# A streaming encoder step on one core: the first MLP matrix as seven block products, rounded sums on GpSimd

## The chip, the cores and the metric

The kernel runs on one core of a Trainium2 chip. The metric is the time of one execution on the device in microseconds (us), median of several runs. In this kernel TensorE multiplies, VectorE and ScalarE do the elementwise work and read TensorE's results from PSUM, GpSimd does elementwise work in SBUF alone, SyncE (SP) issues most transfers; GpSimd issues some.

## The reference

One layer: input LayerNorm, one large projection, a pooling branch and a stick-breaking attention branch, gates, an output projection, a LayerNorm, a squared-ReLU MLP, a last LayerNorm. 512 new frames and 64 frames of a running stream, 576 rows that matter in the MLP. The part that the change touches:

```python
h = _layer_norm(ALPHA * h + (mix @ w_out + b_out), ln1_g, ln1_b)                        # 576 x 1024
f = jnp.square(jax.nn.relu(h @ w_mlp1 + b_mlp1)) @ w_mlp2 + b_mlp2                      # 1024 -> 4096 -> 1024
h = _layer_norm(ALPHA * h + f, ln2_g, ln2_b)
```

## The kernel before

Everything is kept transposed: channels on the 128 partitions, rows along the free axis, in two halves of 288 columns. A float32 operand x is split into a rounded part `hi` (type fp32r, written by ScalarE as a copy or a square) and a remainder `lo` = x - hi (written by VectorE); a product is three matmuls, hi*hi, hi*lo, lo*hi. A **unit** is a block of 128 output channels of a matrix with 1024 input channels: 8 steps x 2 halves x 3 = 48 matmuls. Weight units (512 KB) come by SP into a ring `raw` of four, ScalarE rounds one into `whi`, VectorE writes `wlo`, two units ahead of TensorE at most.

The MLP has 32 hidden units. Each gives a relu (ScalarE, from the PSUM banks `lin`), a square (VectorE), a rounded square (ScalarE) and its remainder (VectorE). The kernel goes through three passes of 12, 12 and 8 units (`PASS_UNITS`). After each of the first two passes, `winograd(s)` multiplies the 12 fresh hidden units with their part of the second matrix: hidden units are taken in six pairs and columns in two halves, so that the hidden activations are 2 x 2 blocks B11, B12 (even unit), B21, B22 (odd unit), and the pair of output blocks costs seven block products instead of eight. The moving operands are B11, B21, B22 and four sums: V5 = B11 - B12, T3 = B22 - B12, V6 = -V5 - B22, V4 = -V6 - B21. The weights' sums are made by VectorE (`weight_sum`). There are four groups (output blocks g and g + 4) of seven products (`OPS`), each of 6 pairs x 3 = 18 matmuls of 288 columns. Results are added by VectorE from PSUM into `r2`, the residual (`add_op`). The last 8 hidden units keep plain `f_hi`, `f_lo`, and the closing stage multiplies them plainly with the last part of the second matrix (`last_products`, weights split by `split_end`), output block by output block, with the last LayerNorm in between.

Order is written out by hand, engine by engine; each engine runs its queue in order, and semaphores hold it where a result is not there. Names in the change: `f_lo_done` counts remainders of hidden operands, `s_hi` and `s_lo` rounded weights and their remainders for the block products, `op_done` finished products, `lo_split` remainders of weight units. SP waits for `s_lo` before it loads over a place. GpSimd sums for the LayerNorms and is idle from 412 us, when it has written two constants, until 759 us. The residual's base (`residual2`, ScalarE) is made between hidden units 4 to 11.

## Time and profile before

| | us |
|---|---|
| median of 3 runs | 806.76 (806.7 to 807.0) |
| span of the profiled execution | 806.8 |
| TensorE (PE) busy | 792.7, 98% |
| VectorE (DVE) busy | 508.3, 63% |
| ScalarE (ACT) busy | 391.6, 49% |
| GpSimd (POOL) busy | 124.7, 15% |

The profiled execution's own time is its span, from the first to the last instruction. Busy time is summed over the whole span; what bounds a stage is read from that stage. Matmuls overlap in the pipeline (a record of 0.30 us, a new one every 0.13 us), so stages are measured from first start to first start. "idle before" is time in which an engine waited just before a group, with what ended it.

### The profile page before, as it was taken

The numbers are of one execution on the slowest core, as the hardware profiler recorded it, in microseconds if no ns is written. First come the engines' busy times: TensorE is split into PE (matmuls) and PEld (weight loads), VectorE is DVE, ScalarE is ACT, GpSimd is POOL, SyncE is SP. The second block draws the span as 40 slices with busy tenths as digits, with TensorE's granted clock in tenths as the row PEclk, the third lists the DMA queues.
The fourth block names the chain that finished last, engine by engine and source line by source line (L and its number), as shares of the span: only waits on it lengthen the run. The fifth ranks groups of instructions, "written<-read, shape, count | busy, mean of one in ns | idle before, by whom it ended". The sixth has DMA issues, their size and how long they took to land.

```text
span 806.8 us, 14570 instructions
## 1 busy us (share of the span) xinstructions
PE 792.7 (98%) x5863; PEld 766.1 (95%) x5864; DVE 508.3 (63%) x857; ACT 391.6 (49%) x652; POOL 124.7 (15%) x170
## 2 busy tenths in 40 slices
PE   8999999999999999999999999999999999999995
PEld 6999899999989999999999999999999999999994
DVE  5833344754547377876877779775667977445644
ACT  4633345655655475562556663334455433345324
POOL 2100000472220110016720000000000000000356
PEclk9999999999999999999999999999999999999998
DMA  7732231112111121243302214222221422222203
GB/s 275 291 116 85 73 113 53 54 56 80 53 54 53 53 70 62 79 131 106 95 11 79 66 39 157 80 105 79 87 75 49 157 79 105 80 78 79 79 2 117
DMA packets 23034, 71.62 MB, mean 89 GB/s; under 512 B 2416, under 2 KB 6656, under 8 KB 22592
## 3 DMA queue, kind: packets, MB, share of 16 engines
q1 hardware_dynamic: 22016, 67.97, 25.8%
q0 software_dynamic: 544, 2.52, 0.9%
q8 instruction: 40, 0.66, 0.3%
q10 hardware_dynamic: 416, 0.33, 0.1%
q14 instruction: 18, 0.15, 0.1%
HBM read 65.96 MB, written 4.85 MB: 88 GB/s over the span
## 4 chain that ended last, share of the span: by engine, by line
PE 93%; ACT 2%; DVE 2%; issue 1%; DMA 1%; SPq 0%; DVEq 0%; ACTq 0%
PE lin L652 15%; PE lin L653 14%; PE lin L654 14%; PE z L1143 6%; PE z L1146 6%; PE z L1145 6%; PE z L908 3%; PE lin L1046 3%; PE lin L1047 2%; PE lin L1048 2%; PE lin L1164 2%; PE lin L1162 2%; PE lin L1163 2%; PE z L973 1%; PE z L654 1%
## 5 line engine op out<-in xcount | busy, mean ns | idle before, releaser
L652 PE MATMUL lin<-h_hi,whi 128*128 128x288 f32 (+1 forms) x832 | 247.5, 297 | 0.0
L653 PE MATMUL lin<-h_lo,whi 128*128 128x288 f32 (+1 forms) x832 | 245.9, 296 | 0.0
L654 PE MATMUL lin<-h_hi,wlo 128*128 128x288 f32 (+1 forms) x832 | 245.0, 294 | 0.0
L652 PEld LDWEIGHTS lin<-h_hi,whi 128*128 128x128 f32 x832 | 156.4, 188 | 1.3 <-issue 1.1
L654 PEld LDWEIGHTS lin<-h_hi,wlo 128*128 128x128 f32 x832 | 156.6, 188 | 0.0
L653 PEld LDWEIGHTS lin<-h_lo,whi 128*128 128x128 f32 x832 | 156.4, 188 | 0.1
L1872 DVE TENSOR_TENSOR wlo<-raw,whi 128x1024 fp32r<-128x1024 f32 x65 | 80.2, 1234 | 33.9 <-ACT whi L1237 29.0
L1237 ACT ACTIVATE whi<-raw 128x1024 fp32r<-128x1024 f32 x58 | 61.0, 1051 | 50.6 <-PE lin L654 32.6
L1659 ACT ACTIVATE relu_t<-lin,vecs 128x288 f32<-128x288 f32 x60 | 30.0, 500 | 91.5 <-PE lin L654 88.1
L2328 DVE TENSOR_TENSOR relu_sq<-relu_t 128x288 f32<-128x288 f32 x60 | 27.4, 456 | 64.4 <-ACT relu_t L1659 64.4
L1143 PE MATMUL z<-f_ops,whi 128*128 128x288 f32 x216 | 64.1, 297 | 0.0
L1146 PE MATMUL z<-f_ops,wlo 128*128 128x288 f32 x216 | 63.5, 294 | 0.0
L1145 PE MATMUL z<-f_ops,whi 128*128 128x288 f32 x216 | 63.1, 292 | 0.0
L1706 ACT ACTIVATE whi<-w_set 128x768 fp32r<-128x768 f32 x36 | 30.5, 846 | 52.2 <-PE z L1146 41.9
L2867 POOL TENSOR_TENSOR sum<-r 128x576 f32<-128x576 f32 x1 | 1.4, 1432 | 347.0 <-DVE r L2568 347.0
L1143 PEld LDWEIGHTS z<-f_ops,whi 128*128 128x128 f32 x216 | 40.6, 188 | 0.4 <-issue 0.4
L2475 DVE TENSOR_TENSOR wlo<-w_set,whi 128x768 fp32r<-128x768 f32 x36 | 34.4, 956 | 10.0 <-ACT whi L1706 9.9
L1145 PEld LDWEIGHTS z<-f_ops,whi 128*128 128x128 f32 x216 | 40.6, 188 | 0.0
L1146 PEld LDWEIGHTS z<-f_ops,wlo 128*128 128x128 f32 x216 | 40.5, 187 | 0.0
L2093 DVE SCALAR_TENSOR_TENSOR sa<-z,sa 128x512 f32<-128x512 f32 (+4 forms) x25 | 19.8, 794 | 25.6 <-ACT sa L1415 25.4
L1145 PE MATMUL z<-f_ops,third_hi 128*128 128x288 f32 x120 | 35.6, 297 | 0.0
L1146 PE MATMUL z<-f_ops,third_lo 128*128 128x288 f32 x120 | 35.6, 297 | 0.0
(360 smaller groups left out, 1920.3 us busy)
## 6 DMA issues: line engine op xcount, KB each, us to landing
raw<-w_stream SPq DMA_DIRECT2D x88, 512.0 KB, 3.5
w_set<-w_sets SPq DMA_DIRECT2D x32, 384.0 KB, 3.7
r<-x_t SPq DMA_DIRECT2D x8, 296.0 KB, 6.2
kcache<-k_cache SPq DMA_DIRECT2D x1, 2048.0 KB, 10.0
vcache<-v_cache SPq DMA_DIRECT2D x1, 2048.0 KB, 8.1
y<-r SPq DMA_DIRECT2D x8, 160.0 KB, 1.8
k_new<-k_t POOLq DMA_DIRECT2D x1, 1184.0 KB, 4.8
v_new<-v_t POOLq DMA_DIRECT2D x1, 1024.0 KB, 5.2
```

The source lines that it names most:

```text
L652: pe.matmul(out, w_h, hi, start=first, stop=False)
L653: pe.matmul(out, w_h, lo, start=False, stop=False)
L654: return pe.matmul(out, w_l, hi, start=False, stop=last)
L1143: pe.matmul(out, w_h, f_op(f, i, 0), start=opens and i == 0, stop=False, skip_group_check=True)
L1145: pe.matmul(out, w_h, f_op(f, i, 1), start=False, stop=False, skip_group_check=True)
L1146: last = pe.matmul(out, w_l, f_op(f, i, 0), start=False, stop=i == PRS - 1, skip_group_check=True)
L1237: nc.scalar.activation(whi[:, j % SPLIT, :], raw[:, j, :], ACT.Copy).then_inc(hi_split, 1)
L1659: nc.scalar.activation(dst, lin[:, bank, 0:HA], ACT.Relu, bias=vec(V_B1 + u)).then_inc(bank_free[bank], 1)
L1706: nc.scalar.activation(op_home(o)[0], w_set[g % 2][:, i, :], ACT.Copy).then_inc(s_hi, 1)
L1872: tt(wlo[:, j % SPLIT, :], raw[:, j, :], whi[:, j % SPLIT, :].bitcast(F32), ALU.subtract)\
L2328: tt(dst, src, src, ALU.mult).then_inc(f_sq_done, 1)
L2475: tt(home[1], w_set[g % 2][:, RAW_SLOT[q], :], home[0].bitcast(F32), ALU.subtract).then_inc(s_lo, 1)
```

## The change

The first 8 hidden units stay as they are. The other 24 are made by seven block products too, in six **sets** of four units; the second matrix for hidden units 0 to 23 goes in six sets as well, each for four output blocks and eight hidden units. The order of the twelve sets is: out 0 (two sets, for the first 8 units), in 1 (two), out 1 (two), in 2, out 2, in 3 ("in": first matrix, "out": second). Then comes the closing stage for the last 8 hidden units as before. One product is 2 output blocks x 4 steps x 3 = 24 matmuls. Its weights are 1024 wide.

```diff
+HIDDEN = 8
+PRS = 4
+OPS = 7
+WU = PRS * 2 * P
+ORDER = (0, 3, 2, 1, 4, 5, 6)
+W_AL, W_SI, W_X, W_DE, W_AP, W_DP, W_GA = range(OPS)
+SETS = [("out", 0, 0), ("out", 0, 1)]
+for _p in (1, 2, 3):
+    SETS += [("in", _p, 0), ("in", _p, 1)] + ([("out", _p, 0), ("out", _p, 1)] if _p < 3 else [])
+N_SETS = len(SETS)
```

TensorE's part; `pair` are two PSUM banks, one of four pairs (the bank `small` joins `z`):

```diff
+            def moving_ready(t, s):
+                kind, p, g = SETS[t]
+                f = MOVING[ORDER[s]]
+                if kind == "in":
+                    if p == 1 and g == 0 and f >= V5:
+                        pe.wait_ge(hs_lo_done, f - V5 + 1)
+                elif p and g == 0:
+                    pe.wait_ge(f_lo_done, tiles_before(2 * p - 1) + LO_ORDER.index(f) + 1)
+            def banks_ready(t, s):
+                ins, outs = sets_before("in", t), sets_before("out", t)
+                was_in = t and SETS[t - 1][0] == "in"
+                if s == 0 and t:
+                    pe.wait_ge(relu_done, 8 * (ins - 1) + 2) if was_in else pe.wait_ge(r_added, 6 * (outs - 1) + 3)
+                elif s == 1 and t and not was_in:
+                    pe.wait_ge(r_added, 6 * (outs - 1) + 5)
+                elif s == 2:
+                    pe.wait_ge(first_copied, t + 1)
+                elif s == 4:
+                    pe.wait_ge(z_summed, 2 * ins + 1) if SETS[t][0] == "in" else pe.wait_ge(r_added, 6 * outs + 2)
+                elif s == 6:
+                    pe.wait_ge(z_summed, 2 * ins + 2) if SETS[t][0] == "in" else pe.wait_ge(r_added, 6 * outs + 4)
+            def block_product(t, s):
+                kind, p, g = SETS[t]
+                o, f = OPS * t + s, MOVING[ORDER[s]]
+                home, (chain, copy, second, third) = op_home(o), bank_pairs(t)
+                pair = (chain, second, chain, copy, chain, third if kind == "in" else second, chain)[s]
+                pe.wait_ge(s_lo, o + 1)
+                banks_ready(t, s)
+                moving_ready(t, s)
...
+                        pe.matmul(out, w_h, hi, start=s < 2 and i == 0, stop=False, skip_group_check=True)
...
+                last.then_inc(op_done, 1)
```

Weights of a set: four blocks by five plain loads of SP, and two of the sums by an accumulating transfer of GpSimd onto a block that has landed (`si_base`, `ap_base`). VectorE makes the other two (`x_sum`, `dp_sum`).

```diff
+            def load_block(t, n, block, landed):
+                sp.dma_start(set_home(n), wsets_d[t, block]).then_inc(landed, 16)
...
+            for t in range(1, N_SETS):
+                a, b, c, d, g = set_slots(t)
+                o = OPS * (t - 1)
+                sp.wait_ge(s_lo, o + W_SI + 1)
+                sp.wait_ge(x_made, t)
+                load_block(t, a, 0, al_in)
+                sp.wait_ge(s_lo, o + W_X + 1)
+                sp.wait_ge(dp_made, t)
+                load_block(t, c, 2, si_base)
+                sp.wait_ge(s_lo, o + W_AP + 1)
+                load_block(t, b, 1, de_in)
+                sp.wait_ge(s_lo, o + W_DP + 1)
+                load_block(t, d, 2, ap_base)
+                sp.wait_ge(s_lo, o + W_GA + 1)
+                load_block(t, g, 3, ga_in)
...
+            def x_sum(t):
+                if t == N_SETS:
+                    return
+                a, _, c, _, _ = set_slots(t)
+                dve.wait_ge(si_in, 16 * (t + 1))
+                tt(set_home(a), set_home(c), set_home(a), ALU.add).then_inc(x_made, 1)
+            def dp_sum(t):
+                a, b, _, _, _ = set_slots(t)
+                dve.wait_ge(x_made, t + 1)
+                tt(set_home(b), set_home(b), set_home(a), ALU.add).then_inc(dp_made, 1)
```

ScalarE, in the order of one set (`block_relu` makes two relus of a block, `block_hi` and `block_plain` its rounded and its plain square, 576 elements each; `set_tail` handles the block that only the last product completes):

```diff
+            def first_copy(t):
+                chain, copy, _, _ = bank_pairs(t)
+                act.wait_ge(op_done, OPS * t + 1)
+                nc.scalar.activation(pair_banks(copy), pair_banks(chain), ACT.Copy).then_inc(first_copied, 1)
...
+            def set_tail(t):
+                block_relu(t, C21)
+                if SETS[t][1] == 3:
+                    block_hi(t, C21)
+                block_plain(t, C21)
+            for t in range(N_SETS):
+                kind, p, g = SETS[t]
+                tail = t - 1 if t and SETS[t - 1][0] == "in" else None
+                o = OPS * t
+                for s in range(OPS):
+                    if s == 0 and tail is not None:
+                        set_tail(tail)
+                        op_hi(o + 2)
+                        continue
+                    if s == 1:
+                        first_copy(t)
+                    if kind == "in" and s == 2:
+                        second_copy(t)
+                    if kind == "in" and s == 4:
+                        block_relu(t, C11)
+                        block_hi(t, C11)
+                        block_plain(t, C11)
+                    if kind == "in" and s == 6:
+                        block_relu(t, C12)
+                        if p == 3:
+                            block_hi(t, C12)
+                        block_plain(t, C12)
+                    op_hi(o + s + 2)
+                    if t == 0 and s == 0:
+                        for f in (V6, T3, V4):
+                            sum_hi(f, PRS - 1)
+                    if kind == "in" and s == 5:
+                        block_relu(t, C22)
+                        block_hi(t, C22)
+                        block_plain(t, C22)
+                    if t == 0 and s < 4:
+                        residual2((4, 0, 2, 6)[s])
+                        residual2((5, 1, 3, 7)[s])
+                    if t == 1 and 1 <= s <= 4:
+                        hs_round(V5 + s - 1)
+            split_end(0)
+            set_tail(N_SETS - 1)
             def first_chunk2(h):
```

VectorE, the same loop, and the sums and remainders that it calls (`third_sum`, `fourth_sum` add two PSUM pairs or a copy for C12 and C22; `out_add` adds a result pair to `r2`, six per "out" set):

```diff
+                if o in HI_ORDER:
+                    dve.wait_ge(f_hi_done, hi_before(m) + HI_ORDER.index(o) + 1)
+                else:
+                    dve.wait_ge(v_rounded, SET_IN + len(ROUND_ORDER) * m + ROUND_ORDER.index(o) + 1)
+                if o in (B11, B22, B21):
+                    dve.wait_ge(plain_done, 4 * m + {B11: 1, B22: 2, B21: 4}[o])
+                src = f_b11[:, :, :] if o == B11 else plain_pairs(o, g)
+                tt(f_pairs(o, g, 1), src, f_pairs(o, g, 0).bitcast(F32), ALU.subtract).then_inc(f_lo_done, 1)
...
+            for t in range(N_SETS):
+                kind, p, g = SETS[t]
+                inner, o = kind == "in", OPS * t
+                tail = t - 1 if t and SETS[t - 1][0] == "in" else None
+                blocks = tail is not None and SETS[tail][1] == 3
+                sums = tail is not None and SETS[tail][1] < 3
+                for s in range(OPS):
+                    if s == 0:
+                        if t and SETS[t - 1][0] == "out":
+                            out_add(t - 1, 5)
+                        if blocks:
+                            last_lo(tail, C12)
+                        if sums:
+                            set_lo(tail, V5)
+                            v_sum(tail, V4)
+                    if inner:
+                        if s == 3:
+                            third_sum(t)
+                        elif s == 5:
+                            fourth_sum(t)
+                            last_lo(t, C11) if p == 3 else set_lo(t, B11)
+                    elif s >= 2:
+                        out_add(t, s - 2)
+                    if s == 6:
+                        x_sum(t + 1)
+                        if inner and p < 3:
+                            v_sum(t, V5)
+                            v_sum(t, T3)
+                    if s == 2:
+                        dp_sum(t)
+                    op_lo(o + s + 2)
+                    if t == 0 and s == 0:
+                        for f in (V6, T3, V4):
+                            sum_lo(f, PRS - 1)
+                    if sums:
+                        for f in {0: (V6,), 1: (B21, T3), 2: (B22,), 3: (V4,)}.get(s, ()):
+                            set_lo(tail, f)
+                    if blocks and s == 0:
+                        last_lo(tail, C21)
+                    if inner and s == 6:
+                        if p == 3:
+                            last_lo(t, C22)
+                        else:
+                            v_sum(t, V6)
+                    if t == 1 and 2 <= s <= 5:
+                        hs_low(V5 + s - 2)
+            split_end(0)
+            last_lo(N_SETS - 1, C12)
+            last_lo(N_SETS - 1, C21)
```

GpSimd, behind the constants of the second LayerNorm: sums of the normed input for the first matrix (`hs_sums`, four operations of 4 x 288 elements, then eight bias additions), then for each set its two transfers and, behind an "in" set of pass 1 or 2, the rounding of five hidden operands:

```diff
+            pool.wait_ge(n1_scaled, 2 * KC)
+            pool.wait_ge(f_lo_done, 11)
+            nc.gpsimd.tensor_tensor(hs_sums[:, V5 - V5, :, :], r1[:, 0:PRS, half(0)], r1[:, 0:PRS, half(1)],
+                                    ALU.subtract).then_inc(hs_made, 1)
...
+            pool.wait_ge(hs_made, 5)
+            for k in range(PRS):
+                hs_shift(T3, k, bias_diff[:, k:k + 1])
+            for k in range(PRS):
+                hs_shift(V6, k, vec(V_LN1_B + PRS + k))
+            def v_round(t, o):
+                _, p, g = SETS[t]
+                m = sets_before("in", t)
+                if o == B21:
+                    pool.wait_ge(plain_done, 4 * m + 4)
+                else:
+                    pool.wait_ge(v_made, 4 * m + (V5, T3, V6, V4).index(o) + 1)
+                nc.gpsimd.tensor_scalar(f_pairs(o, g, 0), plain_pairs(o, g), 1.0, 0.0, ALU.mult, ALU.add)\
+                    .then_inc(v_rounded, 1)
+            for t in range(N_SETS):
+                _, _, c, d, _ = set_slots(t)
+                pool.wait_ge(si_base, SET_IN + 16 * (t + 1))
+                pool.dma_start(set_home(c), wsets_d[t, 3], accum_op=ALU.add).then_inc(si_in, 16)
+                pool.wait_ge(ap_base, SET_IN + 16 * (t + 1))
+                pool.dma_start(set_home(d), wsets_d[t, 0], accum_op=ALU.add).then_inc(ap_in, 16)
+                if t and SETS[t - 1][0] == "in" and SETS[t - 1][1] < 3:
+                    for o in ROUND_ORDER:
+                        v_round(t - 1, o)
```

ScalarE rounds and VectorE subtracts the four `hs_sums` in set 1. `residual2` moves to set 0 and waits for the input sums, since it writes where they are read from. The closing stage takes its steps in the order 0, 1, 2, 3, 4, 6, 5, 7 for the first output block.

## Rows read from the trace of the kernel before

**Rows 1.** The page, part 1: engine busy us (share) x instructions.
```profile
PE 792.7 (98%) x5863; PEld 766.1 (95%) x5864; DVE 508.3 (63%) x857; ACT 391.6 (49%) x652; POOL 124.7 (15%) x170
```

**Rows 2.** Windows: start:end length, busy per engine (instructions), clock, DMA share, GB/s.
```profile
417.40:481.20 63.80, 63.80 (x483) 63.80 (x482) 48.42 (x101) 39.23 (x76) 0.00 (x0) 1.00 0.19 58
481.20:548.50 67.30, 67.30 (x509) 67.11 (x508) 53.50 (x79) 25.77 (x33) 0.00 (x0) 1.00 0.32 108
```

**Rows 3.** TensorE's timeline where stages and units begin: start us, us, instruction.
```profile
417.51 0.30 PE L1046 MATMUL lin<-h_hi,whi 128*128 128x288 f32 x1
...
443.01 0.29 PE L652 MATMUL lin<-h_hi,whi 128*128 128x288 f32 x1
...
481.25 0.29 PE L1143 MATMUL z<-f_ops,third_hi 128*128 128x288 f32 x1
...
548.17 0.30 PE L652 MATMUL lin<-h_hi,whi 128*128 128x288 f32 x1
...
742.57 0.29 PE L1162 MATMUL lin<-f_hi,whi 128*128 128x288 f32 x1
```

**Rows 4.** Groups from 390 us on, shapes apart: count, busy us, mean ns, idle before.
```profile
L1872 DVE TENSOR_TENSOR wlo<-raw,whi 128x1024 fp32r<-128x1024 f32 x28 | 34.2, 1222 | 5.3 <-ACT whi L1742 2.8 <-ACT whi L1237 2.5
...
L1237 ACT ACTIVATE whi<-raw 128x1024 fp32r<-128x1024 f32 x22 | 23.0, 1046 | 0.0
...
L1659 ACT ACTIVATE relu_t<-lin,vecs 128x288 f32<-128x288 f32 x60 | 30.0, 500 | 91.5 <-PE lin L654 88.1 <-PE lin L1048 3.4
...
L1711 ACT ACTIVATE r<-r,b_now 128x576 f32<-128x576 f32 x8 | 6.0, 764 | 0.0
...
L2867 POOL TENSOR_TENSOR sum<-r 128x576 f32<-128x576 f32 x1 | 1.4, 1432 | 347.0 <-DVE r L2568 347.0
```

**Rows 5.** VectorE's timeline behind the first four hidden units.
```profile
433.10 1.22 DVE L1872 TENSOR_TENSOR wlo<-raw,whi 128x1024 fp32r<-128x1024 f32 x1
434.23 1.19 DVE L2333 TENSOR_TENSOR f_ops<-f_sum,f_ops 128x288 fp32r<-128x288 f32 x3
...
438.32 1.22 DVE L1872 TENSOR_TENSOR wlo<-raw,whi 128x1024 fp32r<-128x1024 f32 x1
```

**Rows 6.** Timelines of GpSimd and VectorE in the attention stretch.
```profile
157.08 1.29 POOL L2734 TENSOR_TENSOR win<-win 128x604 f32<-128x604 f32 x1
158.46 0.82 POOL L2739 TENSOR_SCALAR win<-win 128x591 f32<-128x591 f32 x1
...
157.24 2.61 DVE L2134 TENSOR_TENSOR sp_lo<-sa,sp_hi 128x320 fp32r<-128x320 f32 x2
```

**Rows 7.** The same two timelines where the first normalisation is centred.
```profile
381.72 3.29 POOL L2852 TENSOR_TENSOR r<-r,mean 128x288 f32<-128x288 f32 x4 [3.19 <-ACT mean L1601]
...
382.73 1.53 DVE L2297 TENSOR_TENSOR r<-r,z 128x288 f32<-128x288 f32 x4
```

**Rows 8.** GpSimd's groups of the whole span, shapes apart.
```profile
L2813 POOL TENSOR_SCALAR u_hi<-u_t 128x512 fp32r<-128x512 f32 x4 | 2.5, 619 | 7.5 <-PE small L988 7.5
...
L2668 POOL TENSOR_TENSOR wlo<-raw,whi 128x1024 fp32r<-128x1024 f32 x1 | 2.4, 2369 | 3.4 <-DVE wlo L2023 3.4
...
L2902 POOL TENSOR_SCALAR r<-r,vecs 128x256 f32<-128x256 f32 x2 | 1.1, 556 | 0.2
```

**Rows 9.** The page, part 6: DMA issues, KB each, us to landing.
```profile
w_set<-w_sets SPq DMA_DIRECT2D x32, 384.0 KB, 3.7
...
kcache<-k_cache SPq DMA_DIRECT2D x1, 2048.0 KB, 10.0
...
v_new<-v_t POOLq DMA_DIRECT2D x1, 1024.0 KB, 5.2
```

**Rows 10.** TensorE's last matmuls, and the window around their end.
```profile
796.56 0.61 PE L1194 MATMUL z<-sq,inv 128*128 128x256 f32 x2
...
796.00:800.00 4.00, 1.15 (x4) 0.59 (x4) 2.64 (x8) 2.29 (x6) 2.50 (x4) 0.92 0.00 0
```

**Rows 11.** VectorE's remainder of the first closing unit.
```profile
738.36 1.23 DVE L1882 TENSOR_TENSOR wlo<-raw,whi 128x1024 fp32r<-128x1024 f32 x1 [0.42 <-ACT whi L1253]
```

More of the change, by code:

```diff
@@ L70, in f_order, with hi_before, tiles_before @@
     return out + [(V6, PRS - 1), (T3, PRS - 1), (V4, PRS - 1)]
-F_AT = [{f: n for n, f in enumerate(f_order(s))} for s in range(2)]
+F_AT = {f: n for n, f in enumerate(f_order())}
 F_TILES = 7 * PRS
-PAIR_AT = (0, 3, 1, 2, 4, 5)
+PAIR_AT = (0, 3, 1, 2)
+PAIRS_OF = (slice(0, 4, 3), slice(1, 3))
+HI_ORDER = (B11, B22)
+ROUND_ORDER = (V5, V6, B21, T3, V4)
+LO_ORDER = (B11, V5, V6, B21, T3, B22, V4)
+C11, C22, C12, C21 = range(4)
+def hi_before(m):
+    return F_TILES + 2 * min(m, 4) + 4 * max(m - 4, 0)
+def tiles_before(m):
+    return F_TILES + OPS * min(m, 4) + 4 * max(m - 4, 0)
 V_BIN, V_PSCALE, V_BOUT = 0, 32, 36
@@ L1155, in last_products @@
+            for t in range(N_SETS):
+                for s in range(OPS):
+                    block_product(t, s)
             def last_products(home, m, c, out, ready=None, between=None):
-                for k in range(KC):
+                order = (0, 1, 2, 3, 4, 6, 5, 7) if ready is not None else range(KC)
+                for k in order:
                     if ready is not None:
@@ L1687, in tile @@
                 act.wait_ge(f_sq_done, n - 1)
[L1688 to L1689 removed]
+                relu(u, relu_t[:, h, :], h)
+                if h and u % 2 == 0:
                     return
[L1691 to L1692 removed]
+                act.wait_ge(bank_free[h], N_MLP1 + u + 1)
+                out = f_op(B22 if h else (B11, B21)[u % 2], u // 2, 0)
@@ new lines, in block_relu @@
+            def block_relu(t, c):
+                _, p, g = SETS[t]
+                m = sets_before("in", t)
+                home = block_home(p, g, c)
+                chain, copy, _, third = bank_pairs(t)
+                if c == C22:
+                    act.wait_ge(z_summed, 2 * m + 2)
+                else:
+                    act.wait_ge(op_done, OPS * t + {C11: 4, C12: 6, C21: 7}[c])
+                if m and p < 3 and c in (C11, C12):
+                    act.wait_ge(v_made, 4 * (m - 1) + (1 if c == C11 else 2))
+                    act.wait_ge(f_lo_done, tiles_before(m - 1) + 1)
+                for j in range(2):
+                    u = HIDDEN * p + 4 * g + 2 * j + int(c in (C22, C21))
+                    src = home[:, j, :] if c == C22 else one_bank({C11: copy, C12: third, C21: chain}[c], j)
+                    nc.scalar.activation(home[:, j, :], src, ACT.Relu, bias=vec(V_B1 + u),
+                                         scale=-1.0 if c in (C22, C21) else 1.0).then_inc(relu_done, 1)
+                act.wait_ge(relu_done, 8 * m + 2 * c + 2)
@@ new lines, in out_add @@
+            def out_add(t, n):
+                _, p, g = SETS[t]
+                base = 6 * sets_before("out", t)
+                chain, copy, second, _ = bank_pairs(t)
+                right, h, pair, after, op = ((1, 1, second, 2, ALU.subtract), (0, 1, chain, 3, ALU.add),
+                                             (0, 0, copy, 4, ALU.add), (1, 1, chain, 5, ALU.subtract),
+                                             (0, 1, second, 6, ALU.add), (1, 0, chain, 7, ALU.subtract))[n]
+                m = 4 * right + 2 * g
+                if t < 2:
+                    dve.wait_ge(r2_based, (2, 4, 4, 4, 4, KC)[n] if t == 0 else KC)
+                dve.wait_ge(op_done, OPS * t + after)
+                if n in (3, 4):
+                    dve.wait_ge(r_added, base + n - 2)
+                elif n == 0:
+                    dve.wait_ge(r_added, base)
+                tt(r2[:, m:m + 2, half(h)], r2[:, m:m + 2, half(h)], pair_banks(pair), op).then_inc(r_added, 1)
@@ new lines, in third_sum @@
+            def third_sum(t):
+                chain, _, second, third = bank_pairs(t)
+                m = sets_before("in", t)
+                dve.wait_ge(op_done, OPS * t + 3)
+                if m and SETS[t - 1][0] == "in":
+                    dve.wait_ge(relu_done, 8 * m)
+                else:
+                    dve.wait_ge(r_added, 6 * sets_before("out", t))
+                dve.wait_ge(second_copied, m + 1)
+                tt(pair_banks(third), pair_banks(chain), second_home(t), ALU.add).then_inc(z_summed, 1)
@@ new lines, in _ @@
+            for u in range(4, HIDDEN):
+                n = U_MLP1 + u + 1
+                if u + 1 < HIDDEN:
+                    split(n // 4, n % 4)
+                else:
+                    op_lo(0)
+                    op_lo(1)
+                    x_sum(0)
+                if u % 2 == 0:
+                    for o in (V6, T3, V4):
+                        sum_lo(o, u // 2 - 1)
+                else:
+                    sum_lo(V5, u // 2)
+                tile(u, 0)
+                tile(u, 1)
```

555 lines of the change are left out of this document (279 added, 276 removed).

## The prediction

> **What bounds the kernel now.** I read the page first: TensorE is busy for 98% of the span [rows 1]. The table by stage then shows no gap: in both a plain stretch and a block-product stretch of the MLP TensorE is busy for all of it at clock 1.00, VectorE for 76 to 80% and ScalarE for 38 to 61% [rows 2]. TensorE's own timeline gives the pitch: 504 matmuls of 288 columns from 481.25 to 548.17 us are 66.92 us, 0.1328 us each; the 480 from 417.51 to 481.25 give the same [rows 3]. So each matmul removed from 417 to 743 us is worth 0.133 us, as long as nobody else is late. The rest of the work is to find who is.
>
> **What it removes.** 24 hidden units cost 24 x 48 = 1152 matmuls; six new sets of seven products with 24 matmuls each cost 1008. The second matrix keeps 1008 (six such sets instead of 2 x 4 x 7 x 18). 144 x 0.1328 = 19.1 us less on TensorE. One set is 168 x 0.1328 = 22.31 us, one product 3.19 us; set 0 is due at 417.51 + 288 x 0.1328 = 455.76 (half of units 0 to 3, all of 4 to 7), and the closing stage, which starts at 742.57 [rows 3] and ends with the span, at 723.5.
>
> **What it adds in a steady set.** Consecutive instructions overlap a little: three 288-element VectorE operations take 0.37 us apart, a 1024-element one 1.14 [rows 5]; so I charge 0.67 for 576 elements. ScalarE's 1024-element rounding is 1.05, a relu from PSUM 0.50, 576 elements about 0.7 [rows 4]. A set of the first matrix asks of ScalarE 7 x 0.95 + two PSUM copies 1.4 + eight relus 3.2 + six squares 3.8 = 15 us of 22.3: it fits. VectorE: nine 1024-element operations 10.3, two PSUM sums 1.3, four sums of squares 2.7, seven remainders 4.7: 19 us. It fits too, but the last squares exist only after the set's last product, so the sums and remainders fall into the first third of the next set, in front of that set's weight remainders. Walking the queues in their written order, each product's result 0.2 us after its end, times from the next set's start. ScalarE: the fourth product's block is squared twice before it rounds for the product after next, that rounding ends at -6.2, VectorE's sum for C22 follows at -4.3, C22's relu and squares end at -2.2, C12's at -0.6, the rounding for product two at 0.4, C21's at 1.9. VectorE: sum V5 at 0.1, T3 0.8, the remainder for product two 1.9, sum V6 2.6, V5's remainder 3.3, sum V4 4.0, the remainder for product three 5.1, V6's remainder 5.8, and it has caught up by the fifth product. Without GpSimd this costs some 0.5 to 0.75 us where the next set multiplies these very sums (twice), nothing elsewhere.
>
> **Edits at nothing.** The eight base sums of the residual move from between the hidden units to set 0: 8 x 0.67 us on ScalarE, which holds its rounding for product four until 6.9 us of the set, due at 9.6 less a remainder of 1.2. In set 1 ScalarE rounds the four input sums (1152 elements, 1.24 each by the same pitch) and VectorE makes their remainders (1.27 each): its load is 19.4 of 22.3 us, and the walk puts each weight remainder at least 1 us ahead of its product, since this set has no sums of squares. The second matrix's six adds per set (0.67) replace seven single ones. The queue of SP waits for the remainder that frees each place; the last load of a set is issued near 17.4 us, lands before its end, and is wanted by the next set's fifth product. Of the four weight sums of a set VectorE keeps two; the accumulating transfers make the others. If these covers went, the first to be late would be the sum that feeds product three, since SP's next base load and GpSimd's transfer queue behind it.
>
> **GpSimd beside VectorE.** This is the term that decides. In the attention stretch two 320-element VectorE subtractions, 0.4 us apart if free, took 2.61 us: each stood behind one whole GpSimd instruction (157.08 and 158.46), and GpSimd's next in turn behind it [rows 6]. Where VectorE reads one operand from PSUM, four operations beside four of GpSimd took their usual 1.53 us [rows 7]. So operations with both inputs in SBUF alternate with GpSimd, whole instruction by whole instruction. The Trainium skill says the same (SBUF — State Buffer, Who interferes with whom): a VectorE instruction with two SBUF inputs contends with a GpSimd one that reads SBUF, and the later one waits until the first is done. By that rule, the trace agrees with 2.61 us for two operations; by it the sum below has 7.4 and 10.3 us where a view of the engines as independent would have 0.8 and 1.5.
>
> Rounding: GpSimd takes 0.62 us for 512 elements [rows 8], so 0.69 for 576, five times after each first-matrix set of passes 1 and 2, just in that crowded third. Alternating, VectorE's queue in the next set becomes: V5's remainder 3.9 us, the third weight remainder 6.9, V6's 8.2, the fourth weight remainder 10.0, B21's and T3's 11.3, the sum for the sixth product 12.4, the fifth remainder 13.6, B22's 14.2. Next set of the second matrix: product two is due at 3.2 and starts at 3.9, product three waits for V6 until 8.3 (due 7.1), product five for the add that frees its bank until 15.7 (due 14.7): 2.9 us. Next set of the first matrix: product three waits until 7.0 (due 6.4), product five for its sum in PSUM until 15.0 (due 13.4): 2.2 us. Two of each: 10.3 us, of which 1.5 remain without GpSimd.
>
> **The start.** GpSimd makes the four sums of the normed input. They may start when the eleventh remainder is written, at 433.1, the time of VectorE's weight remainder for unit 5 [rows 5]. Four operations of 1152 elements: 1024 took 2.37 and 576 1.43 us [rows 8, 4], so 2.65 each; then eight bias additions of 288 elements, 0.45 each (256 elements 0.56, 512 0.62 [rows 8]). VectorE has seven short operations between the remainders of units 5 and 6 (434.23 to 438.32 [rows 5]), all from SBUF. Alternating: 434.2 + 4 x 2.65 + 4 x 0.45 + 7 x 0.37 + 1.14 = 450.4 us. TensorE needs that remainder when unit 6 starts, at 443.01 [rows 3]: a stall of 7.4 us. What is late next: GpSimd is through at 453.3, its first accumulating transfer lands near 459, and set 0, pushed to 463.2, needs the matrix at 466.4: covered by the stall. Free of any collision the terms would be: GpSimd through at 448.5, transfer at 454, product three waits for V6 and the copy until 462.9 instead of 462.1: 0.8 us. I take 7.4, the alternation, since [rows 6] shows it; both ends stay for the range. The clock: the last matmuls end at 797.2, and the granted clock averages 0.92 over 796 to 800, which is full clock until about 799.4 and 0.5 (1.2 GHz) after it [rows 10]: it fell some 2 us after TensorE went quiet. A gap of 7.4 us is longer, so TensorE would come back at the lower level; no row shows for how long. Each us there loses at most half a us; I take 1.7, between none and 3.4.
>
> **The end.** Now the first closing unit is split under the last hidden units (its remainder is written at 738.36, 4.2 us before it is needed [rows 11, 3]). In the new order its rounding stands behind the last set's relus and squares: ScalarE gets to it at -0.1 us, VectorE finishes at 2.2, so TensorE stands 2.3 us; the last block's remainders (3.8) are covered by the six k steps before them. The rest of the closing stage is unchanged.
>
> **DMA.** Per set five plain loads of 512 KB and two that GpSimd issues with accumulation, each after a plain load of the same place. A plain 384 KB load lands in 3.7 us; a GpSimd-issued 1 MB store in 5.2 [rows 9]. No accumulating one is in the trace: between these 3.7 and the 10.0 of the 2 MB load. I take 5.5, near the GpSimd row. The chain sum, load, accumulation, next sum then has 6.0 to 6.7 us for the accumulation in the crowded sets and over 8.5 in the others: hidden.
>
> **Sum.** -19.1 + 7.4 + 1.7 + 10.3 + 2.3 = +2.6 us on a profiled span of 806.8, which equals the median of the runs (806.76): 809.4.
>
> **Rivals.**
> 1. The collisions cost less than the walk says (rounds fall beside VectorE's PSUM operands or its waits). None at all: 806.8 - 19.1 + 0.8 + 1.5 + 2.3 = 792.3. Only the start's: 800.6; only the rounds': 801.1. For it: VectorE is idle a quarter of the time [rows 2]. Against: both places are where its queue is fullest.
> 2. The accumulating transfer is slow. At 10 us it pushes the sum X, with V5 behind it, by 3.3 us in two sets and by about 1 in four more: 819. It decides from 6.7 us on. For it: reading and writing the same place; against: 5.2 us for twice the bytes.
> 3. The matmuls' gain does not come (pitch over 0.133 through changing banks): nothing in the trace shows it; each 0.001 us is 2 us.
>
> **Chances.** As walked 0.48 (its own range 804 to 815), rival 1 0.37, rival 2 0.12, rival 3 0.03. Range 792 to 819. A difference under 0.2% (1.6 us) can't be told from none here. Faster: rival 1 and a tenth of the first: 0.41; same 0.13; slower 0.46.
>
> **What would show it.** TensorE idle near 443 us, waiting for a weight remainder, with GpSimd rows of 2.7 us and VectorE rows of 3; a PEclk below 1 just behind. Waits for remainders of f in the products two, three and five of the sets that follow one of the first matrix, and VectorE rows of 576 elements at 1.3 us beside GpSimd's. About 2.3 us before the closing stage. It is wrong if unit 6 starts at 443, if these rows keep 0.75 us, or if VectorE waits for the accumulating queue.

## The result, and the profile after

The changed kernel takes 813.2 us (median of four runs, 812.5 to 818.3), the one before 806.7: ratio 1.0091 (1.0075 to 1.0107), slower by 6.5 us by the medians; 809.4 was forecast. A run's time stands 1.7 us above its span (first to last instruction). The page of before shows an execution with a span of 806.8; its later executions have 804.0 to 806.6, with 805.1 near the middle, so spans compare as 805.1 to 811.1.

The page, part 1, answers to [rows 1]:

```profile
PE 779.1 (96%) x5720; PEld 750.2 (92%) x5720; DVE 533.2 (66%) x749; ACT 415.8 (51%) x646; POOL 195.2 (24%) x227
```

143 matmuls fewer are recorded, so the gain is there, but TensorE is no longer busy all the time. The head of the list of TensorE's waits from 417 to 760 us (what it waited for: us in total, times, longest), where before had none at all:

```profile
PE lin L755 <- DVE wlo L2080: 5.2, 1, 5.2
PE z L1272 <- DVE f_ops L2749: 4.4, 3, 2.0
PE z L1272 <- DVE wlo L2677: 2.8, 2, 2.6
PE lin L1289 <- ACT f_last L1878: 2.3, 1, 2.3
PE z L1272 <- DVE z L2707: 1.1, 1, 1.1
PE lin L1272 <- DVE z L2707: 1.1, 1, 1.1
...
```

L2080 is the remainder of a weight unit, L2749 that of a hidden operand after a first-matrix set, L2677 that of a set's weights, L2707 the sum that frees product five's banks; L1289 is the closing stage. (The wait of L1289 is put down to L1878; what ended it was the closing unit's remainder, written at 746.63.) A gap is measured here from one matmul's start to the next, less the usual pitch of 0.133. All of them: 5.4 us ahead of unit 6; 0.2 inside set 0's product two and 2.8 ahead of its product three; 2.1, 0.6 and 0.8 ahead of products two, three and five of each second-matrix set that follows a first-matrix one; 0.3 and 1.3 ahead of three and five of each first-matrix set that does; 2.5 ahead of the closing stage. That is 21.1 us, and two stretches at half clock add 3.7. With -19.1 the sum is +5.7. The account closes in the other runs too: in each of the thirteen traces of the changed kernel and its variants, the span less its gaps and its half clock is 785 to 787 us, beside 805.1 - 19.1 = 786.0.

**The start.** Timeline of GpSimd, then of VectorE (start, us, instruction; xN merges N):

```profile
432.34 3.61 POOL L3167 TENSOR_TENSOR hs_sums<-r 128x1152 f32<-128x1152 f32 x1 [20.67 <-DVE f_ops L2541]
435.90 2.89 POOL L3169 TENSOR_TENSOR hs_sums<-r 128x1152 f32<-128x1152 f32 x1
...
444.55 7.44 POOL L3163 TENSOR_SCALAR hs_sums<-hs_sums,bias_diff 128x288 f32<-128x288 f32 x4
451.97 5.62 POOL L3163 TENSOR_SCALAR hs_sums<-hs_sums,vecs 128x288 f32<-128x288 f32 x4
457.54 0.93 POOL L3197 DMA_DIRECT2D raw<-w_sets  x1
```
```profile
433.32 8.64 DVE L2541 TENSOR_TENSOR f_ops<-f_sum,f_ops 128x288 fp32r<-128x288 f32 x3
441.89 2.86 DVE L2536 TENSOR_TENSOR relu_sq<-relu_t 128x288 f32<-128x288 f32 x1
444.79 0.64 DVE L2541 TENSOR_TENSOR f_ops<-relu_sq,f_ops 128x288 fp32r<-128x288 f32 x1
445.35 0.44 DVE L2536 TENSOR_TENSOR relu_sq<-relu_t 128x288 f32<-128x288 f32 x1
...
446.21 1.22 DVE L2080 TENSOR_TENSOR wlo<-raw,whi 128x1024 fp32r<-128x1024 f32 x1
```

Four VectorE operations stand behind four sums, 2.9 us each where [rows 5] had 0.4. Beside the bias additions VectorE has its usual 0.44 or 0.2 more, and it is GpSimd that is slow: 1.25 to 2.6 us an addition. The last two took 1.25 each, although VectorE stood idle during the first of them, so that is their own price. So an addition lasts 1.25 us and more, but holds VectorE for only 0.2: here VectorE does not wait for the whole instruction, as the prediction's rule has it. GpSimd comes to its first transfer at 457.5 instead of 453.3; it lands at 463.07. VectorE, whose next remainder needs it, stands idle for 5.3 us until 464.16 and is then behind with the work for product three.

The clock (windows: start:end, length, busy per engine, granted clock, DMA share, GB/s) in the gap ahead of unit 6 and behind it, behind set 0's gap, and in a gap of 2.2 us:

```profile
441.97:447.48 5.51, 0.29 (x4) 0.06 (x2) 5.44 (x6) 1.12 (x3) 5.40 (x3) 0.79 0.00 0
447.48:451.96 4.48, 4.48 (x18) 4.48 (x19) 4.41 (x9) 3.11 (x7) 4.48 (x3) 0.50 0.34 117
451.96:456.00 4.04, 4.04 (x32) 4.04 (x32) 2.69 (x6) 0.94 (x2) 4.04 (x4) 1.00 0.43 134
...
471.80:475.92 4.12, 4.12 (x19) 4.12 (x20) 3.37 (x5) 4.12 (x6) 0.00 (x0) 0.59 0.68 240
...
560.66:562.86 2.20, 0.29 (x4) 0.10 (x2) 2.20 (x4) 1.65 (x3) 0.74 (x1) 1.00 0.79 145
```

Half clock (1.2 GHz) for 4.5 us with 18 matmuls in place of 33, full behind it; 3.7 us lost in both stretches.

**A set after a first-matrix set.** GpSimd and VectorE where set 4 begins (second matrix, from 557.5):

```profile
549.01 0.89 POOL L3197 DMA_DIRECT2D raw<-w_sets  x1 [7.19 <-DMA raw<-w_sets]
...
559.20 1.11 POOL L3191 TENSOR_SCALAR f_ops<-f_plain 128x576 fp32r<-128x576 f32 x1 [1.03 <-DVE f_plain L2726]
562.12 4.99 POOL L3191 TENSOR_SCALAR f_ops<-f_plain 128x576 fp32r<-128x576 f32 x4 [1.82 <-DVE f_plain L2731]
```
```profile
557.21 1.23 DVE L2663 TENSOR_TENSOR raw<-raw 128x1024 f32<-128x1024 f32 x1 [3.19 <-DMA raw<-w_sets]
558.35 0.75 DVE L2726 TENSOR_TENSOR f_plain<-f_b,f_b 128x576 f32<-128x576 f32 x1
559.02 0.75 DVE L2728 TENSOR_TENSOR f_plain<-f_plain,f_b 128x576 f32<-128x576 f32 x1
559.69 1.69 DVE L2677 TENSOR_TENSOR wlo<-raw,whi 128x1024 fp32r<-128x1024 f32 x1
561.30 0.74 DVE L2731 SCALAR_TENSOR_TENSOR f_plain<-f_plain 128x576 f32<-128x576 f32 x1
561.97 0.74 DVE L2749 TENSOR_TENSOR f_ops<-f_plain,f_ops 128x576 fp32r<-128x576 f32 x1
562.63 1.21 DVE L2736 SCALAR_TENSOR_TENSOR f_plain<-f_plain 128x576 f32<-128x576 f32 x1
```

The transfer issued at 549.01 lands at 557.21, after 8.2 us; VectorE had been idle for 3.2. For the last 0.9 of them, from 556.3 when ScalarE's square of C12 ended, it could have made the sums V5 and T3 (L2726, L2728), but they are queued behind the weight sum X (L2663), which needs the transfer. TensorE, due at 560.8, gets V5's remainder at 562.7. Rows of 1.69 and 1.21 are the collisions: 0.47 above 1.22 and 0.74, one for each rounding.

### The profile page after: what moved, and what is told of

The parts are those of the page before. It is cut to its first block, busy times and chain, and to the rows that moved or that the text cites. A ratio compares the mean times of both kernels' runs of the same rounds, so it can differ in the third digit from the quotient of the medians.

```text
span 811.1 us, 14048 instructions
## 1 busy us (share of the span) xinstructions
PE 779.1 (96%) x5720; PEld 750.2 (92%) x5720; DVE 533.2 (66%) x749; ACT 415.8 (51%) x646; POOL 195.2 (24%) x227
## 4 chain that ended last, share of the span: by engine, by line
PE 74%; DVE 8%; ACT 5%; DMA 4%; issue 4%; POOL 3%; SPq 0%; DVEq 0%; ACTq 0%; POOLq 0%
PE lin L755 7%; PE lin L756 7%; PE lin L757 7%; PE z L1272 6%; PE z L1273 5%; PE z L1274 5%; DMA raw<-w_sets 4%; PE z L1011 3%; PE lin L1149 2%; PE lin L1150 2%; PE lin L1151 2%; PE lin L1289 2%; PE lin L1290 2%; PE lin L1291 2%; PE lin L1272 2%
## 5 line engine op out<-in xcount | busy, mean ns | idle before, releaser
L755 PE MATMUL lin<-h_hi,whi 128*128 128x288 f32 (+1 forms) x448 | 134.9, 301 | 5.2 <-DVE wlo L2080 5.2
L756 PE MATMUL lin<-h_lo,whi 128*128 128x288 f32 (+1 forms) x448 | 133.5, 298 | 0.0
L757 PE MATMUL lin<-h_hi,wlo 128*128 128x288 f32 (+1 forms) x448 | 133.0, 297 | 0.0
L755 PEld LDWEIGHTS lin<-h_hi,whi 128*128 128x128 f32 x448 | 85.2, 190 | 6.7 <-DVE wlo L2080 5.4
L756 PEld LDWEIGHTS lin<-h_lo,whi 128*128 128x128 f32 x448 | 85.2, 190 | 0.1
L757 PEld LDWEIGHTS lin<-h_hi,wlo 128*128 128x128 f32 x448 | 85.2, 190 | 0.0
L1843 ACT ACTIVATE whi<-raw 128x1024 fp32r<-128x1024 f32 x48 | 50.7, 1057 | 59.5 <-DMA raw<-w_sets 23.2
L2677 DVE TENSOR_TENSOR wlo<-raw,whi 128x1024 fp32r<-128x1024 f32 x48 | 62.3, 1297 | 18.1 <-ACT whi L1843 18.1
L2080 DVE TENSOR_TENSOR wlo<-raw,whi 128x1024 fp32r<-128x1024 f32 x41 | 51.1, 1247 | 28.6 <-ACT whi L1365 26.6
L1365 ACT ACTIVATE whi<-raw 128x1024 fp32r<-128x1024 f32 x38 | 40.0, 1053 | 50.6 <-PE lin L757 32.6
L2677 DVE TENSOR_TENSOR third_lo<-raw,third_hi 128x1024 fp32r<-128x1024 f32 x24 | 31.1, 1298 | 7.2 <-ACT third_hi L1843 7.1
L1272 PE MATMUL z<-hs_hi,whi 128*128 128x288 f32 x96 | 28.5, 297 | 1.3 <-DVE z L2707 1.1
## 6 DMA issues: line engine op xcount, KB each, us to landing
kcache<-k_cache SPq DMA_DIRECT2D x1, 2048.0 KB, 10.2
```

The costliest lines, as they stand in the source:

```text
L755: pe.matmul(out, w_h, hi, start=first, stop=False)
L756: pe.matmul(out, w_h, lo, start=False, stop=False)
L757: return pe.matmul(out, w_l, hi, start=False, stop=last)
L1272: pe.matmul(out, w_h, hi, start=s < 2 and i == 0, stop=False, skip_group_check=True)
L1365: nc.scalar.activation(whi[:, j % SPLIT, :], raw[:, j, :], ACT.Copy).then_inc(hi_split, 1)
L1843: nc.scalar.activation(op_home(o)[0], set_home(source_slot(t, s)), ACT.Copy).then_inc(s_hi, 1)
```

## The experiments

All are edits of the changed kernel; ratios are to the kernel before, run beside them. Where a run is said to be so many us less than the changed kernel, its ratio is taken from the changed kernel's 1.0091, and each ratio has 0.1 to 0.2% (some 1 us) to either side. One of the changed kernel's four times, 818.3, stands far out; by the medians these differences are 0.4 to 1.1 us smaller (8.4, 3.1, 2.9, 5.0 and 11.9 us where 8.8, 4.2, 3.5, 5.9 and 12.9 are given). A gap in a trace is that of one execution: the two gaps ahead of product two in the second-matrix sets are 2.1 and 2.1 us in the changed kernel's, and 3.0 to 5.2 together in the other traces with accumulating transfers, the old order and GpSimd's roundings.

**Roundings on ScalarE.**
```diff
-                nc.gpsimd.tensor_scalar(f_pairs(o, g, 0), plain_pairs(o, g), 1.0, 0.0, ALU.mult, ALU.add)\
+                nc.scalar.activation(f_pairs(o, g, 0), plain_pairs(o, g), ACT.Copy).then_inc(v_rounded, 1)
```
(V5's behind the last block's square, V6's, B21's, T3's and V4's behind the weight roundings that follow.)

> The five roundings after each first-matrix set of passes 1 and 2 go from GpSimd to ScalarE (5 x 0.69 us in the next set, four times); everything else is as in the changed kernel (813.2 us, sets that follow a first-matrix set 3.5, 3.5, 1.6 and 1.6 us late). Theory A, the prediction's: these delays are VectorE taking turns with GpSimd, so all but 1.5 of 10.3 us go: 804.4. Theory B, read from the trace after: the 2.07 and 2.14 us ahead of product two in the second-matrix sets come from the accumulating transfer, which landed only 8.2 to 8.4 us after its issue, and stay; the rest (0.62 + 0.79, 0.65 + 0.74, 2 x 1.6 = 6.0) goes at most: 807 to 809. Theory C: ScalarE, with 18.5 of 22.3 us then, is late itself and nothing is gained: 812 to 815. VectorE's rows of 576 elements at 1.21 and of 1024 at 1.68 go back to 0.75 and 1.22 in all of them.

Measured 804.8 us, 0.9982 (0.9969 to 0.9996): faster than before, 1.09% or 8.8 us less than the changed kernel. Its waits from 417 to 760 us:

```profile
PE lin L755 <- DVE wlo L2097: 5.2, 1, 5.2
PE z L1272 <- DVE f_ops L2766: 2.5, 2, 2.1
PE z L1272 <- DVE wlo L2694: 2.5, 1, 2.5
PE lin L1289 <- ACT f_last L1878: 2.3, 1, 2.3
```

The gaps of products three and five are gone, all 6.0 us; product two's are 2.3 and 0.5. So the trace has theory B's picture, and the median theory A's size. In its own profiled execution (802.3) also the half clock of set 0 is missing (1.6 us); how much of the 8.8 is clock can't be told from one trace, and this one is the fastest of ten (the median is 804.8).

**Bias additions folded** into ScalarE's rounding and VectorE's remainder:
```diff
-            for k in range(PRS):
-                hs_shift(T3, k, bias_diff[:, k:k + 1])
+                    nc.scalar.activation(hs_hi[:, o - V5, k, :], hs_sums[:, o - V5, k, :], ACT.Identity,
+                                         bias=bias_diff[:, at:at + 1]).then_inc(hs_hi_done, 1)
```

> The eight bias additions of GpSimd (444.6 to 457.5 us in the trace after) are left to ScalarE's rounding (as its bias) and VectorE's remainder (as its scalar), eight more short instructions for each in set 1; the four sums of 1152 elements stay. Theory A: TensorE's 5.4 us stall ahead of unit 6 is due to the four sums alone and stays, the first accumulating transfer is issued near 446 instead of 457.5 and lands before set 0, and the 0.2 + 2.8 us ahead of products two and three of set 0 go, with the 1.6 us at half clock behind them: 813.2 - 4.6 = 808.6. Theory B: the additions hold VectorE as well, so that unit 6 comes earlier too: 806 to 808. Theory C: set 0 was late for its long queues on VectorE and ScalarE and not for the transfer: 812 to 813.5.

810.2 us, 1.0039 (1.0025 to 1.0053): 4.2 us less than the changed kernel. Set 0 has no gap left, unit 6 still waits 4.9 us: theory A. The time is 1.6 us above the 808.6 of that theory. (One product two was 3.7 us late in its trace, with 1.5 us of half clock behind it, and 1.3 us more were lost so in the closing stage.)

**First closing unit early**, ahead of block C22 on both engines:
```diff
+                    if t == N_SETS - 1 and s == 5:
+                        split_end(0)
                     if kind == "in" and s == 5:
                         block_relu(t, C22)
...
-            split_end(0)
             set_tail(N_SETS - 1)
```

> The first closing unit is rounded and its remainder made before the last two blocks of the last set are squared (ScalarE's 1.05 and VectorE's 1.23 us move ahead of C22's). Theory A: the 2.50 us ahead of the closing stage go, and C12's remainder still comes within the six k steps before it is needed: 810.8. Theory B: the last blocks are late in its place and 1 us or more stays: 812.

810.3 us, 1.0048 (1.0031 to 1.0065): 3.5 us less. The 2.5 us ahead of the closing stage are gone, 0.9 come back inside it: its seventh step needs C21, not C12 as the expectation had it, and C21 is the last product's block. The time is theory A's (810.8), but the closing stage without a wait that belongs to it did not come. The trace has a new gap of 1.4 us in set 1 that no run explains.

**Plain transfers:**
```diff
-                pool.dma_start(set_home(c), wsets_d[t, 3], accum_op=ALU.add).then_inc(si_in, 16)
+                pool.dma_start(set_home(c), wsets_d[t, 3]).then_inc(si_in, 16)
```
(and the same for the second one.)

> The two transfers that GpSimd issues per set overwrite their place instead of adding to it, so half of two weight sums is left out; the issue, the queue and the bytes are the same. Theory A, the prediction's: the accumulating transfers are hidden: 813. Theory B: adding is what makes them land after 5.5 us (first) and 8.2 to 8.4 us (sets that follow a first-matrix set); a plain one lands in 3.7 us or so, the 2.07 and 2.14 us ahead of product two go and of the 2.8 us in set 0 1.8: 807. Theory C: they are slow since other loads share the DMA engines, not for adding: landing stays at 8 us and the time at 812 to 813.

808.2 us, 1.0018 (1.0008 to 1.0027): 5.9 us less. Time from issue to landing (min/median/max) of the first kind of transfer, in the changed kernel and here:

```profile
DMA to landing us min/median/max: 5.5/8.1/9.4
```
```profile
DMA to landing us min/median/max: 3.6/5.9/7.4
```

Product two's gaps are 0 and 1.2 instead of 2.1 and 2.1, set 0's 0.7 instead of 2.8. Of the second kind of transfer, accumulating ones land after 5.2/5.4/7.3 us and plain ones after 3.3/3.9/5.0. Theory B, with 1.2 us less gain than it had; and even plain ones of the first kind take 5.9 us here, not the 3.7 assumed. That other loads beside them cause this was not tried. (The trace is the fastest of ten runs, 805.3; most took 808.)

**Sums in pieces** (biases folded, each of the four sums as four of 288):
```diff
+            for k in range(PRS):
+                hs_piece(V5, k, r1[:, k, half(1)], r1[:, k, half(0)], ALU.subtract)
```

> As the run with the bias additions folded in (810.2 us; 4.9 us stall ahead of unit 6), and GpSimd's four sums of 1152 elements (2.7 to 2.9 us each beside VectorE) are cut into 16 of 288 (some 0.75 us each, from 576 in 1.43). Same bytes and arithmetic. Theory A, turns by whole instruction: VectorE's eight operations up to unit 6's remainder each stand behind one piece of about 0.75 us instead of 2.8 us, unit 6's remainder ends near 442.5, the stall is 0.7 us or less and the 2.3 us at half clock behind it go: 803 to 805. Theory B: GpSimd keeps VectorE out for as long as it has work, however it is cut: the stall stays near 5 us and the time at 810 or above.

807.1 us, 1.0006 (0.9990 to 1.0021). VectorE's timeline, to set beside the 8.64 and 2.86 above:

```profile
433.38 3.03 DVE L2547 TENSOR_TENSOR f_ops<-f_sum,f_ops 128x288 fp32r<-128x288 f32 x3
436.33 1.07 DVE L2542 TENSOR_TENSOR relu_sq<-relu_t 128x288 f32<-128x288 f32 x1
...
440.27 1.83 DVE L2086 TENSOR_TENSOR wlo<-raw,whi 128x1024 fp32r<-128x1024 f32 x1
...
449.88 1.21 DVE L2086 TENSOR_TENSOR wlo<-raw,whi 128x1024 fp32r<-128x1024 f32 x1
```

Unit 6's remainder ends at 442.1 (442.5 forecast) and unit 6 starts on time: each VectorE operation waits for one whole sum of GpSimd, of whatever length (0.6 us behind 288 elements, 2.5 behind 1152). Theory A's mechanism; its time (803 to 805) was missed, since the pieces go on to 449.6 and unit 7 is 2.5 us late in unit 6's place; one product two is 3.3 us late besides, and 4.3 us are lost at half clock in three places.

**Sums on VectorE**, biases folded:
```diff
                 tile(u, 0)
+                if u == 4:
+                    dve.wait_ge(f_lo_done, 11)
+                if u < HIDDEN - 1:
+                    hs_sum(u - 4)
                 tile(u, 1)
+            hs_sum(3)
```

> As the run with the bias additions folded in, and the four sums are VectorE's (4 x 1.27 us, one in each of units 4 to 7), so that GpSimd does nothing but issue transfers there. Theory A: VectorE is busy for 30 of 38.8 us from 417 on, finds room for 5 us, and TensorE has no stall: 813.2 - 5.4 - 2.2 - 3.0 - 1.6 + at most 1 = 801 to 802. Theory B: VectorE's queue is too full there without GpSimd too, and TensorE waits 2 us or more for a remainder: 804 to 806.

801.3 us, 0.9931 (0.9915 to 0.9947), theory A. TensorE waits for nothing from 417 to 480 us. The start with its consequences cost 1.60% or 12.9 us; the trace of the changed kernel has 8.4 us of gaps and 3.7 of half clock for it.

**V5, T3 and DP early** on VectorE:
```diff
                     if s == 6:
-                        x_sum(t + 1)
                         if inner and p < 3:
                             v_sum(t, V5)
                             v_sum(t, T3)
+                        x_sum(t + 1)
...
-                    if s == 2:
+                    if s == 2 and not sums:
                         dp_sum(t)
                     op_lo(o + s + 2)
+                    if s == 1 and sums:
+                        dp_sum(t)
```

> The changed kernel with two changes of order on VectorE: sums V5 and T3 ahead of the weight sum X (which waits for the accumulating transfer), and in a set that follows a first-matrix set the weight sum DP one place earlier, ahead of B21's and T3's remainders, so that SP's base load and GpSimd's transfer behind it are issued some 1.4 to 2.4 us earlier. Theory A: product two of the second-matrix sets was 2.07 and 2.14 us late through the transfer and V5's remainder behind it; 1.34 us go by the first change and the rest by the second, 0.3 us or less stays, the rest of the delays (0.6 to 0.8 and 1.3) as they are: 809. Theory B: the transfer takes as much longer as it is issued earlier, since the DMA engines are the limit: 811 to 813.

814.5 us, 1.0100 (1.0084 to 1.0117): nothing gained. Product two's gaps fall from 2.1 to 1.1, as the first half should have it, but in the first-matrix sets products two and three are now 0.5 to 0.8 us late, behind DP's 1.2 us: DP was not free to move, which neither theory had.

**All together** (the edits of roundings, biases, sums on VectorE, closing unit and early sums):

> All of it together: roundings on ScalarE, biases folded in, input sums on VectorE, first closing unit rounded early, V5, T3 and DP early. If the terms add up, of the 25 us lost between 417 and 747 in the changed kernel 1 to 3 stay (about 0.9 us in the closing stage for C12, some tenths of a us in product two of the second-matrix sets): before's 806.9 - 19.1 + 1 to 3 = 789 to 791. Rival: ScalarE, with 18.5 of 22.3 us and roundings in its fullest third, or VectorE with the input sums at the start, becomes late in their place and 5 us or more stay: 793 or above.

791.8 us, 0.9820 (0.9806 to 0.9834), 0.8 above the range given and below the rival's. 3.9 us of gaps are left where 1 to 3 were expected; with them the sum is 806.9 - 19.1 + 3.9 = 791.7, so the terms add up.

**The same without the early sums** (their diff undone):

> As the run with all of it (791.8 us), without the two changes of order on VectorE (V5 and T3 behind the weight sum X again, DP in its old place). Theory A: product two of the two second-matrix sets is 2.2 us late each again, as it was with the roundings on ScalarE alone (2.26), instead of 1.15: about 2 us more, 793 to 794.5. Theory B: the changes of order are worth nothing here either, as in the run that had them alone (814.5 beside 813.2): 791.5 to 792.

790.9 us, 0.9796 (0.9782 to 0.9809), the lowest of all, though its interval touches those of the other orders, so that it is no faster for certain: theory B, and 0.6 below its range. The waits of its profiled execution, the slowest of its five (794.2, the others 790.2 to 791.1), are theory A's: product two 1.4 and 2.2 us late, and 1.5 us of half clock behind the second:

```profile
PE z L1273 <- DVE f_ops L2776: 3.3, 2, 2.0
PE lin L1290 <- DVE f_lo L2783: 0.8, 1, 0.8
```

**The last one with the roundings on GpSimd again** (the first diff undone):

> As the run without the reordering, but the five roundings are GpSimd's again: its difference to that run is what the roundings on GpSimd cost where nothing else is late. Theory A (0.47 us for each VectorE operation beside a rounding; 1.4 us in product three and five after the second-matrix tails and 1.6 in the first-matrix ones): 6 us more, 799 to 801. Theory B, the prediction's price (2.9 and 2.2 less 0.75 in each): 8.8 us more, 802 or above.

800.1 us, 0.9912 (0.9897 to 0.9927): 1.16% or 9.4 us more, theory B's size, though the time itself lies in theory A's range. The largest waits from 417 to 760 us:

```profile
PE z L1273 <- DVE f_ops L2759: 3.3, 3, 1.5
PE lin L1273 <- DVE z L2717: 1.1, 1, 1.1
PE z L1273 <- DVE z L2717: 1.1, 1, 1.1
PE lin L1290 <- DVE f_lo L2766: 0.8, 1, 0.8
PE lin L1273 <- issue: 0.6, 1, 0.6
PE z L1273 <- issue: 0.6, 1, 0.6
PE lin L1273 <- DVE f_ops L2759: 0.5, 1, 0.5
...
```

Among these are the changed kernel's delays of products three and five again, 6.1 us as gaps. Its profiled execution is its fastest (797.3, clock 0.996); the others have 0.993 to 0.994 and 800. By that mean clock about 0.25% of 800 us, some 4 us, more of them ran at half speed, worth some 2 us; the rest of the 9.4 isn't placed.

**Two more orders** of the version with all of it: DP back in its place,

> As the run with all of it, but DP back in its old place, so that only V5 and T3 stand ahead of X. Theory A: the base load comes 1 us or so later and the transfer behind it with it, but in the sets that follow a first-matrix set B21's and T3's remainders come earlier: within 1 us of 791.8. Theory B: DP's earlier place is what let the transfer land in time: 793 or above.

791.7 us, 0.9814 (0.9800 to 0.9827), theory A; and V5's rounding ahead of the last block's squares, its remainder ahead of X:

```diff
+                        if sums:
+                            v_round(tail, V5)
                         set_tail(tail)
...
                         if sums:
                             set_lo(tail, V5)
+                            x_sum(t)
                             v_sum(tail, V4)
```

> As the run with all of it, but V5's rounding stands ahead of the last block's squares on ScalarE, and on VectorE V5, T3 and V6 are summed first, then product two's weight remainder and V5's remainder are made, and only then X and V4 are summed; DP in its old place. Theory A: what is left ahead of product two (1.15 and 1.11 us) is VectorE's X (1.14 us) in front of the remainder that product two waits for: it goes but for 0.2, product three may be 0.3 us late: 789.5 to 790.5. Theory B: X comes too late for product three and gives it back: 791 to 792.5.

793.1 us, 0.9822 (0.9808 to 0.9835). Product two's gaps fell to 0.6 and 0.3, but product three of the first-matrix sets is 0.7 late and product five of the second-matrix ones 0.6: theory B's picture, and 0.6 us above its time. VectorE is busy for 7.8 and 7.7 of 8 us in those stretches (525 to 533 and 545 to 553), so each of these orders only chose who was late.

## Why the prediction was right in sign and short in size

- **The matmuls' gain**, 19.1: came. 143 records fewer, pitch 0.133.
- **The start**, 7.4: 5.4. The mechanism was right. The term had four sums at 2.65 us, and four bias additions at 0.45 in front of unit 6's remainder. The sums held VectorE for 2.5 us each, and the additions for 0.2 now and then: 0.6 and some 1.5 us less. The sums in pieces and on VectorE show whose stall it is.
- **"GpSimd is through at 453.3, covered by the stall": the step that failed.** An addition of 288 elements was priced at 0.45 from [rows 8] and took 1.25 to 2.6. The transfer landed at 463.1 instead of 459, and with the stall 2 us shorter set 0 wanted it earlier: 3.0 us of gaps. With the additions folded, the transfer was issued at 445.4, set 0 had no gap, and the kernel gained 4.2 us.
- **The clock**, 1.7: 2.1 behind the start's gap and 1.6 behind set 0's, which was not forecast.
- **The rounds**, 10.3: 10.2 by the gaps, out of other parts: that the total fits is luck. In the sets of the first matrix 1.6 instead of 2.2, in those of the second 3.5 instead of 2.9. 4.2 of the sum are product two's delay, where 1.4 was charged. Most of it is the accumulating transfer: the first kind took 8.1 us in the median against the 5.5 assumed (the second 5.4), over the 6.7 from which rival 2 was to decide; plain transfers took 3.0 of the 4.2 away. Behind it stand V5's remainder and one collision of 0.47. Products three and five, 6.0 in the gaps, are GpSimd's part: 0.47 us for a rounding where 0.69 was charged. Taking the roundings away was worth 8.8 and 9.4 us of time, 8.8 having been forecast; the gaps show only 6.0 of it for certain, so that this size was met is not explained in full.
- **The end**, 2.3: 2.5, and what is late next is C21, 0.9, which the prediction had as covered.
- **Sum:** +2.6 against +5.7 in the trace and 6.5 in the medians. Start -2.0, clock +2.0, set 0 +3.0, end +0.2 make the 3 us between forecast and trace. Rival 1 (collisions cheap) is out as a whole, though a rounding's collision is cheaper than charged; rival 2's mechanism is real and acts beside the forecast one; rival 3 is out. (Rival 2's 819 is 1 us under its own terms, 809.4 + 2 x 3.3 + 4 x 1 = 820.)

## What to carry to other kernels

Before giving an idle engine work beside a busy one, ask which busy engine takes turns with it and how long its single instructions are: a sum of 1152 elements held VectorE for 2.5 us each time, one of 288 for 0.6. The block algorithm's 19 us were real and 16 of them could be had (790.9 us beside 807.2); in the changed kernel they went to GpSimd's sums, bias additions and roundings, to accumulating transfers, and to a closing unit that was split too late. Of these, the additions were priced at a neighbour's row and the transfers at another kind's. Price a helper by a row of its own kind of operands and beside the same traffic, and where a transfer feeds a sum that others queue behind, put an upper bound on its landing.

## What was not expected of the hardware

- GpSimd's tensor_scalar with a scalar from SBUF on 128x288 in place: 1.25 us with VectorE idle for part of it, up to 2.58 beside it; another on 128x256 had 0.56 [rows 8]. Its rounding of 128x576 beside VectorE: 1.1 to 1.6 us, of 128x512 elsewhere 0.62 [rows 8]. Why is open.
- How long GpSimd holds VectorE depends on its operation: per element 2.1 to 2.2 ns for a tensor_tensor (2.5 us by 1152, 0.6 by 288), 0.7 to 0.8 ns for a tensor_scalar (0.47 by 576, 0.2 by 288). A tensor_scalar holds it for much less than its own recorded length (0.2 of 1.25 us and more, 0.47 of 1.1 and more).
- An accumulating transfer of 512 KB from GpSimd, in two places of a set: 5.5 to 9.4 us, 8.1 in the median, and 5.2 to 7.3, 5.4 in the median; overwriting 3.6 to 7.4, 5.9, and 3.3 to 5.0, 3.9.
- Over all profiled executions, 8 of 17 gaps of TensorE of 2.0 to 2.8 us had 3 to 4 us of half clock behind them (1.2 to 1.6 us lost), the others none; what tells them apart is open. All of 3.3 us and more had it.
